# Expert weights loaded in the order in which TensorE reads them

## The reference

```
for i in range(2):
    h = rms_norm(x, norm1_g[i])
    x = x + (conformer_conv(h) if i == 0 else diff_attention(h))
    h = rms_norm(x, norm2_g[i])
    x = x + hierarchical_moe(h)
```

## Time and profile before

| | |
|---|---|
| median of 3 runs | 1757.79 us |
| the profiled execution: its own time, its span | 1766.45 us, 1764.6 us |
| TensorE matmul busy | 1434.9 us (81%) |
| weight loads of TensorE busy | 647.4 us (37%) |
| VectorE, ScalarE, GpSimd busy | 441.5, 328.2, 278.0 us |
| DMA traffic | 473.13 MB, mean 268 GB/s |
| experts of layer 0, from the first up to the last down | 315 to 832 us |
| experts of layer 1 | 1234 to 1741 us |

### The profile page before, as it was taken

The page is one execution under the profiler, slowest core; times in us unless marked ns, Lnnn a source line. Parts: engine busy times, 40 slices in busy tenths (PEclk is TensorE's granted clock), DMA queues, the critical chain, the costliest instruction groups (busy, mean ns, idle before and its releaser), DMA issues.

```text
span 1764.6 us, 16980 instructions
## 1 busy us (share of the span) xinstructions
PE 1434.9 (81%) x6028; PEld 647.4 (37%) x6028; DVE 441.5 (25%) x858; ACT 328.2 (19%) x629; POOL 278.0 (16%) x381
## 2 busy tenths in 40 slices
PE   5995796988877877887699999995987787788783
PEld 3442243332222322332466766653322232232231
DVE  1799414111101101110433433324110101101112
ACT  2555310000000000000334434310100000000000
POOL 0688000111111111111000000001111111111100
PEclk9998786999899989999699999987988989989897
DMA  9022006789999999997800301206889999999995
GB/s 334 13 95 95 0 36 250 286 349 378 413 403 386 410 396 407 398 409 287 330 1 1 144 1 48 96 36 260 342 362 359 397 400 399 405 402 373 411 397 214
DMA packets 91250, 473.13 MB, mean 268 GB/s; under 512 B 19676, under 2 KB 19676, under 8 KB 40261
## 3 DMA queue, kind: packets, MB, share of 16 engines
q1 hardware_dynamic: 78500, 443.12, 62.7%
q0 software_dynamic: 10400, 16.82, 2.6%
q10 hardware_dynamic: 2304, 12.58, 1.8%
HBM read 466.43 MB, written 23.33 MB: 278 GB/s over the span
## 4 chain that ended last, share of the span: by engine, by line
PE 55%; DMA 25%; DVE 7%; SPq 4%; POOL 4%; issue 3%; ACT 1%; ACTq 0%; POOLq 0%; DVEq 0%
DMA ring<-in_moe_w 23%; PE banks L1255 18%; PE banks L1272 8%; PE banks L1364 7%; PE banks L1204 5%; POOL scratch L496 4%; SPq L317 3%; PE banks L1397 3%; PE banks L1153 2%; DVE banks L846 2%; PE banks L1245 1%; PE banks L1458 1%; PE banks L1263 1%; PE banks L1411 1%; PE banks L1438 1%
## 5 line engine op out<-in xcount | busy, mean ns | idle before, releaser
L1255 PE MATMUL banks<-ring,scratch 128*64 128x512 f32 x2016 | 511.8, 666 | 174.9 <-DMA ring<-in_moe_w 164.4
L1255 PEld LDWEIGHTS banks<-ring,scratch 128*64 128x64 f32 x2016 | 159.3, 153 | 524.0 <-issue 523.0
L989 DVE COPY scratch<-banks 128x256 f32<-128x256 f32 x65 | 27.6, 425 | 825.4 <-PE banks L1263 825.4
L1272 PE MATMUL banks<-ring,scratch 128*64 128x512 f32 x976 | 224.6, 602 | 3.0 <-DVE scratch L989 3.0
L661 ACT ACTIVATE scratch<-banks 64x512 f32<-64x512 f32 x65 | 38.3, 589 | 638.0 <-PE banks L1255 638.0
L514 POOL COPY at_out<-rows_out 128x1 int32 (+1 forms) x64 | 11.7, 183 | 752.4 <-ACT scratch L665 752.4
L496 POOL TENSOR_TENSOR scratch<-scratch 128x512 f32<-128x512 f32 x88 | 112.0, 1273 | 62.8 <-ACT scratch L633 50.7
L1364 PE MATMUL banks<-hT,ring 128*128 128x512 f32 x256 | 120.3, 615 | 0.8 <-DVE hT L803 0.8
L1153 PE MATMUL banks<-hT,ring 128*128 128x512 f32 x256 | 113.6, 604 | 0.7 <-issue 0.7
L1272 PEld LDWEIGHTS banks<-ring,scratch 128*64 128x64 f32 x976 | 66.4, 137 | 114.8 <-issue 108.1
L1204 PE MATMUL banks<-ring,area 128*128 128x512 f32 x200 | 99.3, 650 | 10.6 <-ACT area L643 9.6
(11 more groups left out here) (207 smaller groups left out, 1164.0 us busy)
## 6 DMA issues: line engine op xcount, KB each, us to landing
ring<-in_moe_w SPq DMA_DIRECT2D x374, 1024.0 KB, 13.3
area<-in_moe_w SPq DMA_DIRECT2D x12, 1024.0 KB, 15.6
ring<-in_attn_w_qkv SPq DMA_DIRECT2D x12, 1024.0 KB, 15.9
ring<-in_conv_w_in SPq DMA_DIRECT2D x8, 1024.0 KB, 10.8
area<-y_dram ACTq DMA_DIRECT2D x8, 1024.0 KB, 7.9
ring<-in_conv_w_out SPq DMA_DIRECT2D x4, 1024.0 KB
xn_dram<-area ACTq DMA_DIRECT2D x8, 512.0 KB, 2.6
hT<-in_moe_w SPq DMA_DIRECT2D x4, 1024.0 KB, 12.3
```

The source lines that it names most:

```text
L1255: last = mm(bank[2 + s][q * SLOTS:(q + 1) * SLOTS, :], xeT[s][:, j, h, :], w[:, c, :], start=c == 0, stop=c == NC - 1)
L1272: last = mm(bank[6 + s][q * SLOTS:(q + 1) * SLOTS, :], hidT[s][:, j, :], w2c[:, j, q * 512:(q + 1) * 512], start=j == 0, stop=j == 3)
```

## The change

The loads are issued as TensorE reads them: w2(e), w1(e+2), w3(e+2) in the steady loop, which is the order down(e), up(e+2). `load_expert` and `used` are gone; `to_ring(r, src, *free)` puts a unit in ring place r after one wait, `to_extra(k, ...)` puts one in the areas, of which `area2` is now the fourth. The ten units that are loaded ahead become w1 and w3 of experts 0 to 3 and w2 of experts 0 and 1. In the loop w2(e) waits for down(e-2), w1(e+2) and w3(e+2) for up(e). On TensorE up(31) now stands ahead of down(30), and on ScalarE its silu ahead of the copy of y(30). The over tile's three units wait for up(31), down(30) and down(31) (before: up(30), up(30) and down(30)). Behind them three units of the attention's weights are loaded (0, 1, 2; before: unit 3), and units 3, 4, 5 after `y_dram` has been read back. Matmuls, transfers' sizes and all other engines' instructions stay.

```diff
-MOE_UNITS = 3 * (EXPERTS - 1)
+MOE_UNITS = 3 * EXPERTS - 4
...
-                load_expert(0, 0, freed[0:3])
-                load_expert(1, 1, freed[3:6])
-
-                extra_free = ((mix_ready, 8 * (l + 1)), (logits_ready, l + 1), (xn_stored, 16 * NT * (l + 1)))
-                for k, src in enumerate(expert_units(EXTRA)):
-                    sp.wait_ge(*extra_free[k])
...
-                load_unit(flat_halves(ahead_unit), expert_units(EXTRA + 1)[2], unit_loaded[n % RING])
-                load_expert(3, 2, used(1), 2)
-                load_expert(4, 3, used(2))
-                with sp.Fori(2, EXPERTS // 2 - 1) as i:
-                    for s in range(2):
-                        load_expert(i * 2 + (s + 1), s, used(i * 2 + s))
-                load_expert(EXPERTS - 1, EXPERTS - 2, used(EXPERTS - 2))
+                def to_ring(r, src, *free):
+
+                    n = n0 + r
+                    sp.wait_ge(*free)
+                    load_unit(flat_halves(unit(n)), src, unit_loaded[n % RING])
...
+                up, y = main[l]["up_ready"], main[l]["y_ready"]
+
+                to_ring(0, w1_of(0), *freed[0])
+                to_ring(1, w3_of(0), *freed[1])
+                to_ring(2, w1_of(1), *freed[2])
+                to_ring(3, w3_of(1), *freed[3])
+                to_ring(4, w2_of(0), *freed[4])
+                to_ring(5, w1_of(2), *freed[5])
+                to_extra(0, w3_of(2), mix_ready, 8 * (l + 1))
+                to_extra(1, w2_of(1), logits_ready, l + 1)
+                to_extra(2, w1_of(3), xn_stored, 16 * NT * (l + 1))
+                to_extra(3, w3_of(3), xe_loaded[l][1], 16)
+
+                to_ring(6, w2_of(2), up, 1)
+                to_ring(7, w1_of(4), up, 1)
+                to_ring(8, w3_of(4), up, 2)
+                to_ring(9, w2_of(3), up, 2)
+                to_ring(10, w1_of(5), y, 1)
+                to_ring(11, w3_of(5), up, 3)
+                with sp.Fori(1, EXPERTS // 2 - 2) as i:
+                    for s in range(2):
+                        to_ring(3 * s, w2_of(i * 2 + (s + 2)), y, i * 2 + (s + 1))
+                        to_ring(3 * s + 1, w1_of(i * 2 + (s + 4)), up, i * 2 + (s + 3))
+                        to_ring(3 * s + 2, w3_of(i * 2 + (s + 4)), up, i * 2 + (s + 3))
+                to_ring(MOE_UNITS - 2, w2_of(EXPERTS - 2), y, EXPERTS - 3)
+                to_ring(MOE_UNITS - 1, w2_of(EXPERTS - 1), up, EXPERTS - 1)
...
-                    over_tile(0, used(EXPERTS - 1))
+                    over_tile(0, ((up, EXPERTS), (y, EXPERTS - 1), (y, EXPERTS)))
                 meanwhile()
...
+            def first_qkv():
+                sp.wait_ge(done["up_ready"], EXPERTS - 1)
+                qkv_unit(0)
+                sp.wait_ge(done["y_ready"], EXPERTS - 2)
+                qkv_unit(1)
+                sp.wait_ge(done["up_ready"], EXPERTS)
+                qkv_unit(2)
...
-            for n in (0, 1, 2, 4, 5):
+            for n in (3, 4, 5):
                 qkv_unit(n)
...
-                act.wait_ge(y_stored[l][0], 8 * EXPERTS - 16)
-                take_y(m, 0, EXPERTS - 1)
-                silu_of(m, 1, EXPERTS)
+                step(EXPERTS - 1, 1)
...
+                up_step(EXPERTS - 1, 1, in_ring(MOE_UNITS - 4), in_ring(MOE_UNITS - 3))
                 hid_T(m, 0, EXPERTS - 1)
-                down_step(EXPERTS - 2, 0, in_ring(EXPERTS - 3))
-                up_step(EXPERTS - 1, 1, in_ring(EXPERTS - 2))
+                down_step(EXPERTS - 2, 0, in_ring(MOE_UNITS - 2))
                 hid_T(m, 1, EXPERTS)
-                down_step(EXPERTS - 1, 1, in_ring(EXPERTS - 2))
+                down_step(EXPERTS - 1, 1, in_ring(MOE_UNITS - 1))
```

More of the change, by code:

```diff
@@ L59 @@
 MIX_UNITS = (6, 8)
-EXTRA = 2
-MOE_UNITS = 3 * (EXPERTS - 1)
+MOE_UNITS = 3 * EXPERTS - 4
 FIRST = (0, MIX_UNITS[0] + MOE_UNITS)
@@ L132, in trunk @@
         unit_loaded = [sem(f"unit_loaded{i}") for i in range(RING)]
-        extra_loaded = [sem(f"extra_loaded{k}") for k in range(3)]
+        extra_loaded = [sem(f"extra_loaded{k}") for k in range(4)]
         dve_chain, dve_taps = sem("dve_chain"), sem("dve_taps")
@@ L227, in trunk @@
         y_sb = [scratch[:, 4608 + s * 512:5120 + s * 512] for s in range(2)]
-        extra_units = (area3[:], hT[:].rearrange("p c t -> p (c t)"), area1[:])
-        ahead_unit = area2[:]
+        extra_units = (area3[:], hT[:].rearrange("p c t -> p (c t)"), area1[:], area2[:])
         r2 = lambda a, n: scratch[:, 3264 + a:3264 + a + n]
@@ L334, in moe_weights @@
                 w2v = moe_w2[l].rearrange("e (p h j) n -> e h p (j n)", h=2, j=2)
[L336 to L344, removed]
@@ L346, in used @@
-                def used(count):
-                    return [(main[l]["up_ready"], count)] * 2 + [(main[l]["y_ready"], count)]
-                load_expert(0, 0, freed[0:3])
-                load_expert(1, 1, freed[3:6])
-                extra_free = ((mix_ready, 8 * (l + 1)), (logits_ready, l + 1), (xn_stored, 16 * NT * (l + 1)))
-                for k, src in enumerate(expert_units(EXTRA)):
-                    sp.wait_ge(*extra_free[k])
-                    load_unit(flat_halves(extra_units[k]), src, extra_loaded[k])
@@ L358, in moe_weights, with w1_of @@
-                n = n0 + 3 * EXTRA + 2
-                sp.wait_ge(xe_loaded[l][1], 16)
-                load_unit(flat_halves(ahead_unit), expert_units(EXTRA + 1)[2], unit_loaded[n % RING])
-                load_expert(3, 2, used(1), 2)
-                load_expert(4, 3, used(2))
-                with sp.Fori(2, EXPERTS // 2 - 1) as i:
-                    for s in range(2):
-                        load_expert(i * 2 + (s + 1), s, used(i * 2 + s))
-                load_expert(EXPERTS - 1, EXPERTS - 2, used(EXPERTS - 2))
+                def w1_of(e):
+                    return [w1v[e, h] for h in range(2)]
@@ new lines, in w3_of, with w2_of, to_extra @@
+                def w3_of(e):
+                    return [w3v[e, h] for h in range(2)]
+                def w2_of(e):
+                    return [w2v[e, h] for h in range(2)]
+                def to_ring(r, src, *free):
+                    n = n0 + r
+                    sp.wait_ge(*free)
+                    load_unit(flat_halves(unit(n)), src, unit_loaded[n % RING])
+                def to_extra(k, src, *free):
+                    sp.wait_ge(*free)
+                    load_unit(flat_halves(extra_units[k]), src, extra_loaded[k])
@@ L373, in over_tile @@
                     e = sp.value_load(ctl[0:1, bass.ds(j + 1, 1)], min_val=0, max_val=EXPERTS - 1)
-                    for k, w in enumerate(expert_units(e)):
+                    for k, w in enumerate((w1_of(e), w3_of(e), w2_of(e))):
                         if freed:
                             sp.wait_ge(*freed[k])
-                        load_unit(flat_halves(unit(n0 + MOE_UNITS + k)), w, over_w[l] if k < 2 else over_w2[l])
+                        load_unit(flat_halves(unit(n0 + MOE_UNITS + 3 + k)), w, over_w[l] if k < 2 else over_w2[l])
                 with sp.If(n_over > 0):
-                    over_tile(0, used(EXPERTS - 1))
+                    over_tile(0, ((up, EXPERTS), (y, EXPERTS - 1), (y, EXPERTS)))
                 meanwhile()
@@ L427, in qkv_unit @@
             def qkv_unit(n):
-                if n >= 3:
-                    sp.wait_ge(done["up_ready" if n < 5 else "y_ready"], EXPERTS)
                 mix_unit(n0 + n, cols_dram(w_qkv, qkv_cols[n]))
-            moe_weights(0, [(glu_ready, 4)] * 2 + [(glu_ready, 8)] * 2 + [(mix_ready, 8)] * 2, lambda: qkv_unit(3))
+            def first_qkv():
[5 more added lines that the diff above has]
+                qkv_unit(2)
+            moe_weights(0, [(glu_ready, 4)] * 2 + [(glu_ready, 8)] * 2 + [(mix_ready, 8)] * 2, first_qkv)
+            sp.wait_ge(done["y_ready"], EXPERTS)
             sp.wait_ge(moe_over, 1)
@@ L1278, in experts, with in_ring, in_extra, up_step @@
                 n0 = FIRST[l] + MIX_UNITS[l]
[L1280 to L1285, removed]
+                def in_ring(r, i=0):
+                    n = n0 + r
+                    return unit(n), unit_loaded[n % RING], i * 32 + 32 * (n // RING + 1)
+                def in_extra(k):
+                    return extra_units[k], extra_loaded[k], 32 * (l + 1)
+                def up_step(e, s, w1, w3):
+                    pe.wait_ge(w1[1], w1[2])
+                    pe.wait_ge(w3[1], w3[2])
+                    up(m, s, w1[0], w3[0], e + 1).then_inc(m["up_ready"], 1)
                 def rows_step(e, s):
@@ L1290, in rows_step, with down_step @@
                     rows_T(m, s)
-                def down_step(e, s, weights, first=False):
-                    w2, *w2_loaded = weights[2]
-                    pe.wait_ge(*w2_loaded)
+                def down_step(e, s, w2, first=False):
+                    pe.wait_ge(w2[1], w2[2])
                     if not first:
                         pe.wait_ge(m["y_taken"], e - 1)
```

(26 more changed lines are left out.)

## The result

The changed kernel takes 1716.3 us (median of 4 runs, 1712.42 to 1716.74), the kernel before 1757.27 us beside it (4 runs): ratio 0.976, 95% interval 0.9743 to 0.9777, a gain of 41 us. Forecast were 1710.5 us, a gain of 47.3, and a range of 1694 to 1733. The profiled execution took 1716.26 us, span 1714.5.

The account below looks back on a forecast made before the run. The prediction took transfers to bound the experts, with the queue running empty once per expert. Layer 1 at -30.0 and layer 0 at -17.3 us gave -47.3, from 1757.8 to 1710.5 us, range 1694 to 1733.

Parts of the forecast that it names:

- The cause: Experts' loads: w2(e) waits for down(e-2), holding back later loads; about 0.8 and 1.0 us of empty queue per expert.
- The steady loop: Experts from up(8) to up(31): the queue never empties, 418 GB/s, so 15.68 us per expert.
- The start: First experts, layer 1: gaps of 4.4 and 1.7 us remain, yet up(8) starts 13.9 us earlier, at 1331.5.
- the row's 4.7 us: Refill of an emptied queue after down(3): 20.5 us, 15.7 of them data; 2.5 of the rest for start, remainder landing.
- The ends: From up(31) to the last down: 18.4 us in layer 1, 37.3 us in layer 0 with the over tile.
- The collision: End of layer 0: three units of attention weights delay the over tile's scatter, +4 us (bounds 0 and 8).
- the sign named: In layer 0, a scatter of the over tile of 5 to 7 us would show the forecast right.
- The base: Whole kernel: the 47.3 us gain was taken off the median, 1757.8 us, though the profiled execution took 1766.45 us.
- A: Steady loop: part of the dips comes from scatters' and gathers' small pieces; 16.0 us per expert, 1726 us; chance 0.20.
- B: Steady loop: 399 GB/s is the memory's mean, so only start and end gain; 1748 us; chance 0.06.
- D: Steady loop: TensorE at half clock is late with up(e), so the queue empties; no own chance, counted in A.
- C: Steady loop: a never-empty queue with four units outstanding is served slower, 385 GB/s, 1772 us; chance 0.03.

Follow-up runs that it names:

- the run that removes it: Changed kernel with the four areas used a second time as they come free in each layer, the ring going on behind them: 1707.0 us, ratio 0.9712.
- run 9: Not a run number: the words are "a run 9 us slower", the profiled run of the unchanged kernel, 9 us above its median; profiled execution 1766.45 us.
- the shorter up: Kernel before the change with half of up's multiplications left out, loads untouched, results differ: 1694.48 us, ratio 0.9637.

## Why the prediction was right, point by point

- **The cause.** Right, and shown from three sides: an early down fills the queue in the old order (416 GB/s), a late one empties it further (380), and in the new order the loop keeps 419 even with a longer up. One reading was loose: I called the 9.98 us of the earlier trace rows the half clock, but the mean granted clock there is 0.81, so it was at 0.50 in part only. No up of the two kernels takes more than 10.1 us, so one wholly at 0.50 (twice 7.09, an estimate) was never met and stays untested.
- **The steady loop, 15.68 us per expert.** Measured 15.84 and 15.79: 6.4 us of the 46 experts. The rate was right (418 priced, 419 and 418 measured); the step that failed is that the expert's bytes over the mean rate give the pace. The pace is that of the most loaded engine, which carries 3.0 and 2.9 rows of an expert where the mean is 2.2 and 1.9, and the estimate in the table above gives it to 0.01 us.
- **The start.** Up(8) was to come 97.3 us after up(0) in layer 1; it came at 98.8. The gap around down(2) was there, and the run that removes it won 5.4 and 6.6 us of it. By the Trainium skill's fixed cost ("DMA: Bandwidth & Descriptors", "Anatomy of one DMA"), which the page gives for one transfer from GpSimd's queue, not for a refill of six from SP's, it would have been 94.6, an estimate; the row's 4.7 us was the nearer.
- **The ends.** Layer 1: 16.9 us against 18.4 forecast, since up(31) took 7.09 us, at the full clock, and not 8.6. Layer 0: 40.0 against 37.3. The later waits of the over tile were priced right in kind, and its up and down ran partly at the half clock after the wait (8.80 and 5.18 us; 7.11 and 3.67 in the run with the attention's weights late).
- **The collision.** Mis-sized: 1.0 us for 4. The weights were nearly through when the scatter went out (3.25 us, not 7.3; the sign named was 5 to 7). They ran from 799 to 814 us, as forecast; the scatter went out only at 812.5.
- **The base.** In the stages that I priced the forecast was -47.4 us and the two profiles differ by 42.9: 4.5 us of the miss of 6.3 are the terms above. The rest, 2 us, I put down to taking the difference off the median though it was made against the profile of a run 9 us slower; no run shows it.
- **Rivals.** A (small pieces cause dips) fell with the shorter up; it had a grain of truth, not in the rate, but in how the rows are shared among engines. B and D fell. C fell: four units outstanding are served at 419 GB/s.

## What to carry to other kernels

Where a queue is in order, the order of its loads decides which release it hangs on: count, from the release of a place to the need of the next unit, how many microseconds of transfers are still queued, and compare it with the longest step of the reader, at its slow clock. Then look at how a never-empty queue ends: a taper of several microseconds says that the engines are unevenly loaded, and the last one sets every landing.

## What the runs showed of the hardware

- An indirect transfer of 128 partitions is shared out in groups of four neighbouring partitions, which go to eight of the 16 DMA engines in turn, partitions 0 to 63 to one eight and 64 to 127 to the other. No view names the engines, so this is inferred, from the packets' sizes and times and from the pace of three orders of the slots. Rows that fill only every second group of four end the queue on a step of 205 GB/s and make the kernel 15 us slower.
- One core's loads from DRAM in pieces of 1 MB, with the gathered and scattered rows, ran at 418 and 419 GB/s for 330 and 364 us without a pause.
